# Prompt attention scores of dilated groups as two 64-row matmuls on queries read in place

## The chip, the cores and the metric

The kernel runs on one core of a Trainium2 chip. The metric is the device time of one execution in microseconds (us); for the kernel before it is the median of three runs.

## The reference

The program is one step of a small hybrid decoder with two layers, on a prompt of 1024 tokens and on 8 samples of 8 tokens. The first layer has three groups of dilated sliding-window attention (window and dilation 128 and 1, 512 and 4, 2048 and 16; 8 heads of 64 each), joined by their softmax denominators, beside a state-space layer; the second has sliding-window attention with sinks. Normalisations and a feed-forward block stand around both. What the change touches is the prompt's attention of the first layer:

```
def dilated_prompt(q, k, v, dilation, n_steps):
    # (1, T, H, 64) -> dilation sequences of T / dilation tokens
    o, m, l = banded_attn(split(q), split(k), split(v), n_steps)

def banded_attn(q, k, v, n_steps):      # blocks of 128 queries, own and previous key block
    s = einsum('nbqgrd,nbkgd->nbgrqk', qb, kb) * (hd ** -0.5)
    s = where(valid, s, NEG_INF); m = s.max(-1); pexp = exp(s - m); l = pexp.sum(-1)
    o = einsum('nbgrqk,nbkgd->nbqgrd', pexp, vb)
```

## The kernel before

Activations lie with features on the 128 partitions and tokens along the free dimension. Each of the five engines has one program of its own, and semaphores order them. Weights come through one buffer in 111 slots: a DMA on the SP queue, a split into a high and a low half on POOL, three matmuls for each product on PE.

For each of the three groups g0, g1, g2, PE computes values, queries and keys; ACT evicts queries and keys to `XA` (tiles 0 to 3 queries, 4 to 7 keys, two heads of 64 rows in each tile). Then `attend` runs on PE (L816 to L896), ACT (L1261 to L1326) and DVE (L1714 to L1786). It has eight tiles of 128 queries, and in each tile four steps of two heads. A tile has one or two key blocks of 128: in g0 all tiles but the first have two, in g1 they alternate (one, two), in g2 all have one. `prompt_cols` and `key_cols` pick the columns: contiguous in g0, with stride 4 in g1, with stride 8 in g2.

A step k goes through the engines as follows.

- ACT `stage` (from L1266, the copy at L1272): for each of the two heads it copies its 64 rows of the queries, times 1/8, into its own 128-column block of `QST`. The other 64 rows of that block are zero: DVE clears `QST` once (L1957). The staging of the next tile's queries stands between the steps of the present one; the first tile's four steps are staged at once at the start.
- PE `scores` (L822 to L833): it waits for the staged queries and for the mask of step k-2, then runs two matmuls of the full 128 rows (L831), the staged block against a whole key tile, into the two halves of one PSUM bank (bank k % 2).
- DVE: mask added into `sm` (L1755), row maximum, negated (L1760). At a tile's first step it also copies the sums of the last tile into `o_st` (L1726 to L1728), after waiting for the DMA that took the output before; at the third step it scales the last tile's output into `o_st` (L1740), and SP sends that to DRAM.
- ACT `exps` (L1287): exp with the maximum as bias, one instruction and one reading of the sum for each head; then `turned_out` of step k-2 (L1295), which evicts the transposed probabilities.
- PE `turn` of step k-2 (L842): transposes of the probabilities into bank 2 + k % 2; `weigh` of step k-3 (L856): the product with the values, into bank 4.

PE's order in a step is scores(k), turn(k-2), weigh(k-3); ACT's is exps(k), turned_out(k-2), stage. `over_tiles` (L277 to L300) runs the tiles as a hardware loop with its first and last ones written out. The second layer's attention uses the same function with 16 heads and its own staged buffer `QCST`. `block_outputs` (L1028 to L1040), in the state-space layer, alternates full-depth matmuls (L1033) with matmuls on 64 rows in two halves of the array and two banks (L1038); it is not touched.

In g2, SP loads the first keys, mask and values for the samples' attention between the tiles' outputs, after tiles 0, 2 and 4 (L463 to L472); the samples' attention follows the three groups, and waits for their last output.

Of the kernel before, what the change touches and what calls it, by code (L numbers as in the profile page):

```python
# [102 lines left out]
def build(nc, a):  # L103
# [14 lines left out]
    with ExitStack() as ctx:  # L118
# [68 lines left out]
        psum = ctx.enter_context(nc.psum_tensor("psum", [P, 8, 512], F32))  # L187
# [38 lines left out]
        def tiles(t, n):  # L226

            return t[:, :].rearrange("p (n c) -> p n c", n=n)
# [21 lines left out]
        QST, QCST = tiles(q_st, 8), tiles(qc_st, 16)  # L250
# [23 lines left out]
        def value_tile(g, i):  # L274
            return 2 * i[0] + i[1] if g == 1 else i

# [378 lines left out]
        def _(pe):  # L655
# [160 lines left out]
            def attend(g, heads, keys, vals):  # L816

                steps, per_kv = heads // 2, 1 if heads == H_A else 4
                staged = QST if heads == H_A else QCST

                def tile(i, nk, before, after):
                    K = key_cols(g, i, nk)(keys)  # L822

                    def scores(k):
                        pe.wait_ge(q_ready, n_q.add())
                        m = n_mask.add()
                        late(s_masked, m - 2)
                        for hh in range(2):
                            h = 2 * k + hh
                            kt = h // 2 if per_kv == 1 else h // 8  # L830
                            mm = pe.matmul(psum[:, k % 2, hh * 256:hh * 256 + nk * P], staged[:, h, :], K[:, kt],  # L831
                                           start=True, stop=True)
                        mm.then_inc(s_mm, 1)  # L833
# [58 lines left out]
                per = {n_q: steps, n_mask: steps, n_exp: steps, n_ptt: steps, n_pv: steps, n_o: 1}  # L892
                if heads == H_C:
                    per[lo] = 1
                over_tiles(pe, g, per, tile)
# [8 lines left out]
            for g in range(3):  # L904
# [26 lines left out]
                if g:  # L931
                    pe.wait_ge(v_turned, (0, 32, 48)[g])
# [264 lines left out]
        def _(act):  # L1197
# [63 lines left out]
            def attend(g, heads):  # L1261
                steps = heads // 2

                staged = QST if heads == H_A else QCST

                def stage(i, k):  # L1266

                    late(s_mm, n_s.add() - steps)
                    for par in range(2):
                        rows = 64 * (par if heads == H_A else (k // 2) % 2)  # L1270
                        q = prompt_cols(g, i)(XA[:, k:k + 1, :])[64 * par:64 * par + 64]
                        mm = act.activation(staged[rows:rows + 64, 2 * k + par:2 * k + par + 1, :], q, ACT.Copy,  # L1272
                                            scale=HEAD_DIM ** -0.5)
                    mm.then_inc(q_ready, 1)
# [79 lines left out]
            for g in range(3):  # L1354
# [15 lines left out]
                if g == 0:  # L1370
                    act.wait_ge(zeroed, 1)
# [34 lines left out]
            act.wait_ge(zeroed, 2)  # L1406
# [30 lines left out]
            act.wait_ge(zeroed, 3)  # L1437
# [20 lines left out]
            for layer in range(2):  # L1458
                if layer == 1:
# [12 lines left out]
                    act.wait_ge(zeroed, 4)  # L1472
# [143 lines left out]
        def _(dve):  # L1616
# [97 lines left out]
            def attend(g, heads):  # L1714
# [33 lines left out]
                def tile(i, nk, before, after):  # L1748
                    for k in range(steps):
# [5 lines left out]
                        dve.tensor_tensor(out, psum[:, k % 2, :].rearrange("p (h c) -> p h c", h=2)[:, :, 0:nk * P],  # L1755
                                          m.unsqueeze(1).broadcast_to([P, 2, nk * P]), ALU.add).then_inc(s_masked, 1)
# [200 lines left out]
            dve.memset(QST, 0.0).then_inc(zeroed, 1)  # L1957
# [457 lines left out]
```

## Time and profile before

| | us |
|---|---|
| median of three runs | 3750.82 |
| least and greatest | 3748.04, 3753.10 |
| profiled execution, own time | 3750.7 |
| profiled execution, span of its instructions | 3748.9 |
| PE busy | 3316.5 (88%) |
| PE weight loads busy | 3172.7 (85%) |
| DVE, ACT, POOL busy | 1485.0, 906.7, 989.7 |
| DMA | 323.01 MB, 24.8% of 16 engines |

PE is TensorE's matmul row and PEld its weight loads, which overlap; DVE is VectorE, ACT ScalarE, POOL GpSimd, SP the engine that issues the DMAs. The granted clock of TensorE is given as a share of 2.4 GHz; it has two levels, 1.0 and 0.5. A float32 matmul has two records of a load and a matmul each. Ends of matmuls are modelled, so the distance from one start to the next tells more than a record's length.

### The profile page before, as it was taken

The page shows a single profiled execution, that of the slowest core. Times are in us where ns is not written, and L with a number is a line of the kernel's source. Part 1 is how long each engine was busy: PE and PEld are TensorE (multiplying, and loading weights), DVE is VectorE, ACT ScalarE, POOL GpSimd, SP SyncE. Part 2 cuts the span into 40 slices and gives each one's busy share as a digit, 9 for nine tenths or more (in the row PEclk, how much of TensorE's full clock was granted, in tenths as well). Part 3 has the DMA queues.
Part 4 walks back from the last instruction along what each step waited for, and adds up shares of the span by engine and source line. Part 5 has one row for each costly group of instructions (what it writes and reads, how often), then busy time and mean ns, then how long its engine had stood idle before and what let it go on. Part 6 is the DMA issues. An engine that isn't in the chain of part 4 may idle for free.

```text
span 3748.9 us, 50836 instructions
## 1 busy us (share of the span) xinstructions
PE 3316.5 (88%) x21025; PEld 3172.7 (85%) x21025; DVE 1485.0 (40%) x1852; ACT 906.7 (24%) x1876; POOL 989.7 (26%) x226
## 2 busy tenths in 40 slices
PE   4978999984478899999999799887889999999978
PEld 4977987983357799999999698876879999999968
DVE  7714013033452533333334762265154333333474
ACT  3106125061031410000001531275141000000151
POOL 3321230310002233333333333200123333333321
PEclk8989999987688999999999899999799999999989
DMA  2221210348921112222225121100111222222411
GB/s 97 103 72 49 90 66 21 118 151 257 279 70 72 48 72 92 92 92 92 92 92 182 39 78 42 53 1 31 60 66 54 78 78 78 78 78 78 156 36 60
DMA packets 84128, 323.01 MB, mean 86 GB/s; under 512 B 19033, under 2 KB 32153, under 8 KB 66073
## 3 DMA queue, kind: packets, MB, share of 16 engines
q1 hardware_dynamic: 84000, 321.18, 24.8%
q8 instruction: 96, 1.57, 0.2%
q14 instruction: 32, 0.25, 0.0%
HBM read 271.98 MB, written 105.23 MB: 101 GB/s over the span
## 4 chain that ended last, share of the span: by engine, by line
issue 36%; POOL 21%; PE 20%; DMA 15%; DVE 3%; ACT 3%; SPq 2%; POOLq 0%; ACTq 0%; DVEq 0%
DMA w_raw<-in_wall 12%; POOL w_lo L643 12%; PE psum L759 11%; POOL w_hi L641 9%; PE psum L784 3%; PE psum L831 2%; PE psum L856 1%; ACT pr L1287 1%; PE psum L700 1%; DMA v_sb<-in_v 1%; SPq L542 1%; PE psum L1033 1%; PE psum L1038 1%; PE psum L958 1%; PE psum L734 0%
## 5 line engine op out<-in xcount | busy, mean ns | idle before, releaser
L641 POOL TENSOR_TENSOR w_hi<-w_raw,param 128x2184 fp32r<-128x2184 f32 x111 | 427.8, 3854 | 2703.9 <-PE psum L759 2132.0
L759 PE MATMUL psum<-h_hi,w_hi 128*128 128x364 f32 x2832 | 630.7, 331 | 42.1 <-ACT xa L1245 22.8
L759 PE MATMUL psum<-h_lo,w_hi 128*128 128x364 f32 x2544 | 567.1, 331 | 8.3 <-DVE h_hi L1678 8.3
L643 POOL TENSOR_TENSOR w_lo<-w_raw,w_hi 128x2184 fp32r<-128x2184 f32 x111 | 561.7, 5060 | 8.7
L759 PEld LDWEIGHTS psum<-h_hi,w_hi 128*128 128x128 f32 x2832 | 497.6, 190 | 43.8 <-ACT xa L1245 23.1
L759 PE MATMUL psum<-h_hi,w_lo 128*128 128x364 f32 x2304 | 512.4, 331 | 0.0
L2198 DVE TENSOR_TENSOR xa<-xa,psum 128x1092 f32<-128x1092 f32 x256 | 330.4, 1291 | 339.6 <-PE psum L759 339.4
L759 PEld LDWEIGHTS psum<-h_lo,w_hi 128*128 128x128 f32 x2544 | 445.0, 190 | 9.3 <-DVE h_hi L1678 9.0
L759 PEld LDWEIGHTS psum<-h_hi,w_lo 128*128 128x128 f32 x2304 | 403.3, 190 | 0.0
L1560 ACT ACTIVATE tmp<-tmp 128x1092 f32<-128x1092 f32 x64 | 71.5, 1118 | 1261.9 <-DVE tmp L2182 1261.9
L759 PE MATMUL psum<-hid_lo,w_hi 128*128 128x364 f32 x1536 | 339.4, 329 | 0.0
L759 PE MATMUL psum<-hid_hi,w_lo 128*128 128x364 f32 x1536 | 339.4, 329 | 0.0
L759 PE MATMUL psum<-hid_hi,w_hi 128*128 128x364 f32 x1536 | 337.6, 328 | 0.0
L2182 DVE SCALAR_TENSOR_TENSOR tmp<-psum,sq 128x1092 f32<-128x1092 f32 x64 | 82.7, 1295 | 544.0 <-PE psum L759 514.0
L1755 DVE TENSOR_TENSOR sm<-psum,mask 128x512 f32<-128x512 f32 (+1 forms) x160 | 94.4, 590 | 511.0 <-PE psum L831 506.9
L759 PEld LDWEIGHTS psum<-hid_hi,w_hi 128*128 128x128 f32 x1536 | 267.2, 188 | 0.0
L759 PEld LDWEIGHTS psum<-hid_lo,w_hi 128*128 128x128 f32 x1536 | 266.9, 188 | 0.0
L759 PEld LDWEIGHTS psum<-hid_hi,w_lo 128*128 128x128 f32 x1536 | 265.8, 188 | 0.0
L784 PE MATMUL psum<-w_hi,h_hi 128*128 128x256 f32 x648 | 185.1, 286 | 23.2 <-DVE h_lo L1638 21.5
L784 PE MATMUL psum<-w_hi,h_lo 128*128 128x256 f32 x648 | 184.1, 284 | 0.0
L1287 ACT ACTIVATE pr<-sm,stat 128x256 f32<-128x256 f32 (+1 forms) x320 | 147.1, 460 | 95.2 <-DVE stat L1760 49.1
L784 PE MATMUL psum<-w_lo,h_hi 128*128 128x256 f32 x576 | 164.1, 285 | 0.0
(313 smaller groups left out, 4467.5 us busy)
## 6 DMA issues: line engine op xcount, KB each, us to landing
w_raw<-in_wall SPq DMA_DIRECT2D x111, 1092.0 KB, 5.0
kt_sb<-in_kt SPq DMA_DIRECT2D x16, 1024.0 KB, 10.9
out_ovs<-in_v SPq DMA_DIRECT2D x8, 2032.0 KB, 15.6
x_keep<-xa SPq DMA_DIRECT2D x2, 4368.0 KB, 11.8
xd_late<-x_keep SPq DMA_DIRECT2D x2, 4368.0 KB, 14.0
out_oks<-in_kt SPq DMA_DIRECT2D x8, 1008.0 KB, 8.2
out_ovs<-in_v SPq DMA_DIRECT2D x8, 1008.0 KB, 8.8
og<-o_st SPq DMA_DIRECT2D x24, 264.0 KB, 2.0
```

The lines of the kernel that those rows point to most:

```text
L542: sp.dma_start(DM[16 * k:16 * k + 16, :, :], s5_k[:, :, 16 * k:16 * k + P]).then_inc(d_in, 16)
L641: pool.tensor_tensor(w_hi[b][:, :], w_raw[:, :], param[:, C_ONE:C_ONE + 1].broadcast_to([P, SLOT]), ALU.mult).then_inc(hi_made, 1)
L643: pool.tensor_tensor(w_lo[b][:, :], w_raw[:, :], w_hi[b][:, :].bitcast(F32), ALU.subtract).then_inc(split, 1)
L700: mm = pe.matmul(UNIT[m][:, c, :], w[:, kc, m * P:m * P + P], x[:, kc, c * CH:(c + 1) * CH], start=kc == 0 and w is WH and x is XH, stop=k ...
L759: mm = pe.matmul(UNIT[s][:, c, :], w[:, kc, cols], x[:, kc, c * CH:(c + 1) * CH], start=first, stop=last)
L784: mm = pe.matmul(psum[:, 3 * s + c, 0:256], x[:, kc], w[:, kc, :], start=kc == 0 and x is XH and w is WH, stop=kc == KC - 1 and x is XL)
L831: mm = pe.matmul(psum[:, k % 2, hh * 256:hh * 256 + nk * P], staged[:, h, :], K[:, kt], start=True, stop=True)
L1287: mm = act.activation(pr[:, o:o + nk * P], sm[:, o:o + nk * P], ACT.Exp, bias=stat[:, h:h + 1], accum_out=stat[:, 16 + h:17 + h])
L1560: act.activation(TMP[:, m, :], TMP[:, m, :], ACT.Square).then_inc(act_own, 1)
L1755: dve.tensor_tensor(out, psum[:, k % 2, :].rearrange("p (h c) -> p h c", h=2)[:, :, 0:nk * P], m.unsqueeze(1).broadcast_to([P, 2, nk * P]) ...
L2182: dve.scalar_tensor_tensor(chunked(TMP[:, m, :]), UNIT[m], 0.0, chunked(rs2), ALU.max, ALU.mult).then_inc(free[m], 1)
L2198: dve.tensor_tensor(chunked(XA[:, m, :]), chunked(XA[:, m, :]), UNIT[m % 2], ALU.add).then_inc(free[m % 2], 1)
```

## The change

The prompt attention of the three dilated groups no longer stages its queries. The two matmuls of a step take 64 rows each, one the upper and one the lower half of the array, with the queries read from `XA` in place as the stationary operand, strided in g1 and g2. They write two PSUM banks, 0 and 1 in even steps and 5 and 6 in odd ones. The factor 1/8 moves into the mask, which becomes a scalar_tensor_tensor. PE waits no more for staged queries in these groups, DVE no longer clears `QST`, and the counts of the semaphore `zeroed` go down by one. PE's program for these groups is written out over the eight tiles instead of looping; ACT, DVE and SP keep their loops. In g0 PE waits for `k_evict`, since bank 6 is now used. The second layer's attention stays as it is.

```
+        def over_tiles_written_out(g, tile):
+            order = [divmod(t, 2) for t in range(8)] if g == 1 else range(8)
+            nk = [1 + t % 2 if g == 1 else min(t + 1, 2 - g // 2) for t in range(8)]
+            steps = list(zip(order, nk))
+            for t, (i, n) in enumerate(steps):
+                tile(i, n, steps[t - 1] if t else None, steps[t + 1] if t < 7 else None)
...
                     def scores(k):
-                        pe.wait_ge(q_ready, n_q.add())
+                        if heads == H_C:
+                            pe.wait_ge(q_ready, n_q.add())
                         m = n_mask.add()
                         late(s_masked, m - 2)
                         for hh in range(2):
                             h = 2 * k + hh
-                            kt = h // 2 if per_kv == 1 else h // 8
-                            mm = pe.matmul(psum[:, k % 2, hh * 256:hh * 256 + nk * P], staged[:, h, :], K[:, kt],
-                                           start=True, stop=True)
+                            if heads == H_A:
+                                rows = slice(64 * hh, 64 * hh + 64)
+                                mm = pe.matmul(psum[:, 5 * (k % 2) + hh, 0:nk * P],
+                                               prompt_cols(g, i)(XA[:, k:k + 1, :])[rows, 0], K[rows, k],
+                                               start=True, stop=True)
...
-                over_tiles(pe, g, per, tile)
+                if heads == H_A:
+                    over_tiles_written_out(g, tile)
...
-                if g:
+                if g == 0:
+                    pe.wait_ge(k_evict, 8)
+                else:
                     pe.wait_ge(v_turned, (0, 32, 48)[g])
                 attend(g, H_A, XA[:, 4:8, :], V)
...
                 def stage(i, k):
+                    if heads == H_A:
+                        n_s.add()
+                        return
...
-                if g == 0:
-                    act.wait_ge(zeroed, 1)
                 attend(g, H_A)
...
-                        dve.tensor_tensor(out, psum[:, k % 2, :].rearrange("p (h c) -> p h c", h=2)[:, :, 0:nk * P],
-                                          m.unsqueeze(1).broadcast_to([P, 2, nk * P]), ALU.add).then_inc(s_masked, 1)
+                        m = m.unsqueeze(1).broadcast_to([P, 2, nk * P])
+                        if heads == H_A:
+                            dve.scalar_tensor_tensor(out, psum[:, 5 * (k % 2):5 * (k % 2) + 2, 0:nk * P],
+                                                     HEAD_DIM ** -0.5, m, ALU.mult, ALU.add).then_inc(s_masked, 1)
...
             dve.wait_ge(t_parked, 16)
-            dve.memset(QST, 0.0).then_inc(zeroed, 1)
```

## Rows read from the trace of the kernel before

**Rows 1.** Windows of the three stages: length, PE PEld DVE ACT POOL busy, clock, DMA

```profile
300.60:388.70 88.10, 73.02 (x488) 63.96 (x488) 48.83 (x96) 66.15 (x224) 7.48 (x2) 0.98 0.12 42
537.20:627.70 90.50, 82.02 (x416) 60.11 (x416) 42.82 (x96) 68.66 (x224) 7.52 (x2) 0.94 0.14 50
776.20:855.40 79.20, 66.14 (x320) 58.57 (x320) 34.49 (x96) 61.91 (x224) 7.50 (x2) 0.74 0.52 168
```

**Rows 2.** Chain of waits inside g0: start us, length us, what ended last

```profile
356.47 0.93 PE psum L831 x4
357.43 0.70 DVE sm L1755
358.15 0.70 DVE stat L1760
359.97 0.49 ACT pt L1295
360.69 1.10 PE psum L856 x8
```

**Rows 3.** Timeline of the same turn in g0: start, length, engine, instructions

```profile
357.23 0.60 PE L842 MATMUL psum<-ident,pr 128*128 128x128 f32 x4
358.51 1.08 PE L831 MATMUL psum<-xa,q_st 128*128 x4
358.88 0.51 ACT L1287 ACTIVATE pr<-sm,stat 128x256 f32<-128x256 f32 x1 [1.27 <-DVE stat L1760]
```

**Rows 4.** Timeline of ACT at the start of g1

```profile
537.26 3.56 ACT L1272 ACTIVATE q_st<-xa 64x128 f32<-64x128 f32 x8
```

**Rows 5.** Timeline of g1: first scores of three tiles, staging, maximum, exponential

```profile
557.55 1.12 PE L831 MATMUL psum<-xa,q_st 128*128 x4
567.24 2.01 PE L831 MATMUL psum<-xa,q_st 128*128 x4
579.18 1.15 PE L831 MATMUL psum<-xa,q_st 128*128 x4
580.63 1.75 ACT L1272 ACTIVATE q_st<-xa 64x128 f32 x4
581.17 0.42 DVE L1760 TENSOR_REDUCE stat<-sm 128x2 f32<-128x256 f32 x1
582.40 0.40 ACT L1287 ACTIVATE pr<-sm,stat 128x128 f32<-128x128 f32 x1
```

**Rows 6.** Timeline of PE in g2 at the low clock: scores, then transposes

```profile
804.88 1.23 PE L831 MATMUL psum<-xa,q_st 128*128 x4
805.93 0.61 PE L842 MATMUL psum<-ident,pr 128*128 128x128 f32 x2
```

**Rows 7.** Timeline of PE in the block outputs of the state-space layer

```profile
1073.10 0.71 PE L1038 MATMUL psum<-ca,hv 64*128 64x128 f32 x8
1073.75 0.71 PE L1033 MATMUL psum<-d_mat,ut 128*128 128x128 f32 x4
1074.39 0.71 PE L1038 MATMUL psum<-ca,hv 64*128 64x128 f32 x8
```

**Rows 8.** Two groups of the page: line, operation, count, busy us, mean ns

```profile
L2198 DVE TENSOR_TENSOR xa<-xa,psum 128x1092 f32<-128x1092 f32 x256 | 330.4, 1291 | 339.6 <-PE psum L759 339.4
L2182 DVE SCALAR_TENSOR_TENSOR tmp<-psum,sq 128x1092 f32<-128x1092 f32 x64 | 82.7, 1295 | 544.0 <-PE psum L759 514.0
```

**Rows 9.** Weight loads by tile: with stride 32, contiguous; ns least, median, greatest

```profile
L1007 PEld LDWEIGHTS psum<-ident,ub x32: 186/196/231, 1015.9 to 1020.7; 128*128 128x128 f32 x32
L831 PEld LDWEIGHTS psum<-xa,q_st x384: 186/192/338, 301.4 to 849.8; 128*128 128x128 f32 x192
```

**Rows 10.** Timeline of SP and DVE in g2

```profile
828.40 0.43 SPq L400 DMA_DIRECT2D sm_sb<-in_smask  x1
844.07 0.17 DVE L1726 COPY o_st<-stat 128x8 f32<-128x8 f32 x1 [4.32 <-DMA og<-o_st]
```

**Rows 11.** Window at the end of g2, columns as in rows 1

```profile
842.00:857.00 15.00, 7.69 (x40) 7.11 (x40) 4.94 (x15) 5.13 (x22) 0.00 (x0) 0.70 0.12 45
```

More of the change, by code:

```diff
@@ L249, in build @@
         G = param[:, 0:80].rearrange("p (l k c) -> p l k c", l=2, k=5)
-        QST, QCST = tiles(q_st, 8), tiles(qc_st, 16)
+        QCST = tiles(qc_st, 16)
         UNIT = [psum[:, 3 * s:3 * s + 3, 0:CH] for s in range(2)]
@@ L829, in scores @@
                             h = 2 * k + hh
-                            kt = h // 2 if per_kv == 1 else h // 8
-                            mm = pe.matmul(psum[:, k % 2, hh * 256:hh * 256 + nk * P], staged[:, h, :], K[:, kt],
-                                           start=True, stop=True)
+                            if heads == H_A:
[4 more added lines that the diff above has]
+                            else:
+                                mm = pe.matmul(psum[:, k % 2, hh * 256:hh * 256 + nk * P], QCST[:, h, :], K[:, h // 8],
+                                               start=True, stop=True)
                         mm.then_inc(s_mm, 1)
@@ L890, in tile @@
                             outputs_turned()
-                per = {n_q: steps, n_mask: steps, n_exp: steps, n_ptt: steps, n_pv: steps, n_o: 1}
-                if heads == H_C:
-                    per[lo] = 1
-                over_tiles(pe, g, per, tile)
+                if heads == H_A:
+                    over_tiles_written_out(g, tile)
+                else:
+                    over_tiles(pe, g, {n_q: steps, n_mask: steps, n_exp: steps, n_ptt: steps, n_pv: steps, n_o: 1, lo: 1},
+                               tile)
                 pe.wait_ge(o_made, n_o.at)
@@ L1262, in attend @@
                 steps = heads // 2
-                staged = QST if heads == H_A else QCST
                 def stage(i, k):
+                    if heads == H_A:
+                        n_s.add()
+                        return
                     late(s_mm, n_s.add() - steps)
                     for par in range(2):
-                        rows = 64 * (par if heads == H_A else (k // 2) % 2)
+                        rows = 64 * ((k // 2) % 2)
                         q = prompt_cols(g, i)(XA[:, k:k + 1, :])[64 * par:64 * par + 64]
-                        mm = act.activation(staged[rows:rows + 64, 2 * k + par:2 * k + par + 1, :], q, ACT.Copy,
+                        mm = act.activation(QCST[rows:rows + 64, 2 * k + par:2 * k + par + 1, :], q, ACT.Copy,
                                             scale=HEAD_DIM ** -0.5)
@@ L1754, in tile @@
                         m = mask[:, 2 * P:3 * P] if g == 2 else mask[:, 2 * P - nk * P:2 * P]
-                        dve.tensor_tensor(out, psum[:, k % 2, :].rearrange("p (h c) -> p h c", h=2)[:, :, 0:nk * P],
-                                          m.unsqueeze(1).broadcast_to([P, 2, nk * P]), ALU.add).then_inc(s_masked, 1)
+                        m = m.unsqueeze(1).broadcast_to([P, 2, nk * P])
+                        if heads == H_A:
+                            dve.scalar_tensor_tensor(out, psum[:, 5 * (k % 2):5 * (k % 2) + 2, 0:nk * P],
+                                                     HEAD_DIM ** -0.5, m, ALU.mult, ALU.add).then_inc(s_masked, 1)
+                        else:
+                            dve.tensor_tensor(out, psum[:, k % 2, :].rearrange("p (h c) -> p h c", h=2)[:, :, 0:nk * P],
+                                              m, ALU.add).then_inc(s_masked, 1)
                         if k == 0 and before:
```

8 lines of the change are left out of this document (4 added, 4 removed).

## The prediction

> **What bounds the kernel now.** The whole kernel is held by TensorE, but the change lives in three short stages, the prompt attention of the three dilated groups (g0, g1, g2), so only these are read. The first view is the table of windows [rows 1]: the stages last 88.1, 90.5 and 79.2 us, 257.8 us together, and no engine is busy all through. PE comes nearest with 73.02, 82.02 and 66.14 us, but that busy time contains the modelled ends of matmuls. The granted clock is 0.98 and 0.94 in g0 and g1: all but some 3.5 and 11 us at the 2.4 GHz level. In g2 it is 0.74: half of the stage at 1.2 GHz.
>
> The second view is the chain of waits inside g0 [rows 2]. It runs in a circle: scores of a step (L831, 0.93 us), mask (L1755, 0.70), row maximum (L1760, 0.70), two exponentials with their sums on ACT (from 358.87 to 359.97, 1.1), the eviction of an older transposed block (L1295, 0.49, and 0.23 to PE), its product with the values (L856, 1.10), and then the next scores, at 361.79. PE's program puts the product of step k-3 ahead of the scores of step k+1, and ACT's program puts the exponentials of step k-1 ahead of the eviction of step k-3. So one turn of the circle is two steps: 361.79 - 356.47 = 5.32 us. A group has 32 steps, 16 turns; 88.1 / 16 = 5.5 us is the mean turn with its fill and ends. The engines alone would be faster: from the start of a step's transposes over its product to the next scores PE takes 358.51 - 357.23 = 1.28 us [rows 3], with the scores 2.21 a step, 4.42 a turn. Each turn holds the scores once, not twice.
>
> **g0, scores.** The change makes the two matmuls of a step 64 rows deep, in two halves of the array and two PSUM banks. The trace of before has that shape elsewhere: in the block outputs, lines L1033 and L1038 alternate [rows 7]. Two full-depth matmuls (four records) take 1074.39 - 1073.75 = 0.64 us; four matmuls of 64 rows (eight records) take 1073.75 - 1073.10 = 0.65 us, with the same 128 columns. So two halves run in the time of one, and a pair costs half of what it did. Scores fall from 0.93 to 0.46 us. 15 of the 16 turns of g0 have this size (the first tile has one key block): 15 x 0.46 = 7.0 us. The turn stays the limit: about 5.1 us, against 3.5 for PE, 2 x 2 x 0.72 plus 0.5 = 3.4 for DVE, and 3.0 for ACT.
>
> The same rows show a change between 128 and 64 rows every 0.65 us without a gap. The Trainium skill, TensorEngine Tiling (Array Packing), Key Properties, says that changing the tiling mode drains TensorE; by these rows the drain costs nothing that can be seen, and the sum goes by the rows. The case in which it costs is a rival below.
>
> **Staging.** It drops 192 ACT instructions. In g0 they cost nothing but at the start: behind them ACT still waits 1.27 us for DVE [rows 3]. In g1 the queries are read with a stride and a pair costs 0.86 us; two pairs fall together at a tile's start, run from 580.63 to 582.38, and the exponential begins at 582.40 although its maximum was there at 581.17 + 0.42 = 581.59 [rows 5]: 0.8 us late, which I take as 0.75 in each of the four tiles with one key block. In g2 the same block stands before each tile; between 0 (as in g0) and 0.75 I take 0.15 a tile, since there the maximum comes later against the block than in g1. At each group's start eight stagings precede the first exponential: in g1 3.56 us from 537.26 [rows 4]. Without them scores (0.5), mask and maximum (0.45 each) and their hand-overs put it 1.7 us after 537.26, so 1.85 us are gained; the same in g2, and 1.05 in g0, whose stagings are shorter. The memset of the cleared buffer stands ahead of the stage in DVE's program, which then waits for the first scores: 0.
>
> **g1, scores.** Keys are read with a stride there. A step's four records span 2.01 us with 256 columns and 1.12 to 1.15 with 128 [rows 5]; less the 0.15 by which the 1.08 of [rows 3] exceeds the chain's 0.93 [rows 2], scores cost 1.86 and 0.97. A tile with two key blocks takes 579.18 - 567.24 = 11.94 us, one with a single block 567.24 - 557.55 = 9.69 [rows 5]. In the first PE is itself nearly the limit. Halved, its scores are 0.93; the circle then holds, with 0.93 + 0.72 + 0.72 + 1.1, 0.6 for the eviction and 0.9 for a product of one or two key blocks, 5.0 us a turn against 5.97 now: 1.9 us a tile, 7.6 for four. In the second each of two turns loses 0.48, and 0.75 of staging goes: 1.7 a tile, 6.9 for four. Together 14.5 us at the high clock, and 1.85 at the start.
>
> **g2.** A turn loses half of 805.93 - 804.88 = 1.05 us at the low level [rows 6], of 0.97 at the high one: 0.5, so 1.0 a tile, with 0.15 of staging 1.15, 9.2 for eight tiles, and 1.8 at the start. A DMA gives part back: after tile 4 the SP queue issues the sample's mask and values, from 828.40 on, tile 5's output goes behind them, and DVE stands still for it until 844.07 [rows 10]. These 15.6 us stay whatever the engines do, so what is saved on the 1.6 tiles between, about 1.8 us, only makes the wait longer. Downstream nothing swallows the rest: DMA share is 0.12 in the 15 us at the end of g2 [rows 11], and the DMA-heavy sample stage behind it starts when g2's last output lands.
>
> **The clock.** Shorter scores leave PE less to do per us. g2, with the smallest matmuls, is already at the low level for half of its time, g0 and g1 hardly ever [rows 1]. I take g0 as unchanged. In g1 I take a third at the low level: a step with transposes and products of two key blocks is then PE's own, 0.53 + 2.56 = 3.1 us (double of the 1.28 of [rows 3]) against 2.0, 4 us a tile, and 0.7 us for a tile of the other kind; a third of 4 x 4.7 is 6.3. In g2 I take all of it at the low level, 0.5 us a tile more than the mix of today: 2.4 in the parts not held by the DMA.
>
> **Edits with one answer.** The mask becomes a scalar_tensor_tensor with the scale in it: the page has both forms at 1092 columns, 1295 against 1291 ns [rows 8], so 0; bounds 0 and, if 0.1 us in each of 48 turns, 5 us. The stationary operand is read with stride 4 or 8: loads with stride 32 took 196 ns in the median, the contiguous ones of the staged queries 192 [rows 9]: 0. PE's program is written out: the block outputs of [rows 7] are written out too and run without a gap, so fetching costs nothing, and the turns of the loop may be gained, at most the 0.23 us ahead of a product [rows 2] once a tile: 0 to -5, taken as 0. k_evict counts copies that DVE makes before it comes to the stage: 0. Behind PE's dropped wait for staged queries stood the transposes and products of older steps; they now wait for the mask alone.
>
> **Sum.** g0 -7.0 - 1.05 = -8.0; g1 -14.5 + 6.3 - 1.85 = -10.0; g2 -9.2 + 1.8 + 2.4 - 1.8 = -6.8. Together -24.8 us, set against the profiled execution's 3750.7 us (span 3748.9 and 1.8 around it, next to the median 3750.82): 3726 us. With no clock lost, and 2 us of loop turns, it is -35.5: 3715; with half of g1 low, 0.05 us for each switch and each mask: 3738.
>
> **Rivals.**
> - The clock falls in g0 too, and in all of g1: slower. For it: g2, the lightest stage, keeps falling [rows 1]. Against it: g0's transposes and products stay twice as large as g2's. At the low level PE is the limit in g0: 0.93 + 2.56 = 3.49 us a step against 2.55 in my forecast and 2.75 now; 32 x 0.74 - 1.05 = +22.6 us against now. g1 low throughout is 12 against 9.7 us in one kind of tile and 9.6 against 11.9 in the other, so only its start's -1.85 is left; g2 -6.8. Sum +14: 3765. It decides when 26 of g0's 32 steps run low (24.8 / 0.94), with g1 as forecast; 16 to 24 of them give 3741 to 3749.
> - The halves don't overlap where keys are strided. The operands of [rows 7] are contiguous; if the strided read is limited for the array as a whole, scores keep their 0.97 and 1.86 us. Then g0 -8.0, g1 -4 x 0.75 - 1.85 = -4.9, g2 -1.2 - 1.8 = -3: 3735. If no pair overlaps at all, g0 keeps only its start: 3742.
> - Each switch of depth waits for the array to empty. The tail of the last record is 0.07 us in [rows 7] (0.71 less 0.64) and 0.15 in the scores (1.08 less 0.93, [rows 2, 3]); at 0.11, one or two in each of 48 turns are 5 to 10 us: 3731 to 3736. The page's rule on draining (the Trainium skill, TensorEngine Tiling (Array Packing), Key Properties) says this; the seamless cadence of [rows 7] speaks against it.
> - The change doesn't do what it says to the circle: a link that I can't see (the mask on two banks, say) grows by what the scores lose, and only starts are left: 3746.
>
> **How the numbers follow.** About 0.2% (7.5 us) is what a measurement of this kernel can tell from no change: below 3743.3 is faster, above 3758.3 slower. Forecast 0.62; no overlap 0.12 (strided 0.08, none 0.04); draining 0.07: these are faster, 0.81. The clock low in part of g0 0.08 and the unseen link 0.04 are within 0.2%: 0.12. The clock low in all of g0 and g1, 0.07, is slower. The range takes in the forecast's own 3715 to 3738, draining and both kinds of no overlap, and half of the partly low clock: 3713 to 3747.
>
> **What would show it.** In the changed profile the four records of a step's scores should span about 0.5 us in g0 and g2 and 0.95 in g1's larger tiles; a turn in g0 should be near 5.1 us; ACT should have no L1272 in these stages; the stages should last about 80, 80 and 72 us with granted clocks near 1.0, 0.8 and 0.55; DVE's wait for the output's DMA in g2 should grow from 4.3 to about 6 us. The forecast is wrong if records of the two halves follow one another, if g0's granted clock is under 0.9, or if a turn in g0 stays above 5.4 us at the high clock.

## The result, and the profile after

The change makes the kernel slower. The median is 3787.32 us (12 executions, 3756.15 to 3793.90) against 3750.57 us for the kernel before beside it (12, 3747.16 to 3756.52); the ratio is 1.0072, 95% interval 1.0044 to 1.0099. The forecast was 3726 us, in 3713 to 3747. The ratios here are of means. The changed kernel's executions come at two times some 30 us apart, five of these 12 at 3756 to 3763 us and seven at 3785 to 3794, and what divides them is part of the explanation.

The profiled execution took 3793.68 us (span 3791.9). The windows of its three stages, with the columns of [rows 1], from the end of ACT's last eviction to the end of DVE's last output:

```profile
299.32:416.02 116.70, 114.62 (x488) 91.08 (x488) 49.49 (x96) 48.76 (x161) 7.51 (x2) 0.51 0.09 32
566.21:665.94 99.73, 96.86 (x416) 77.27 (x416) 43.20 (x96) 43.62 (x160) 7.53 (x2) 0.52 0.13 45
815.82:893.16 77.34, 70.59 (x320) 57.06 (x320) 34.58 (x96) 36.36 (x160) 7.53 (x2) 0.52 0.51 172
```

The last column but two is what to see: the granted clock is 0.51 and 0.52 in all three stages, 1.2 GHz almost throughout, where it was 0.98, 0.94 and 0.74. g0 grew by 28.6 us and g1 by 9.2; g2 lost 1.9. ACT is busy for 17 to 26 us less a stage, as the staging went, and the stages don't show it. The chain of waits in g0 (start, length, what ended last) answers [rows 2]:

```profile
355.40 1.16 PE psum L840 x4
356.56 1.04 PE psum L855 x4
357.61 1.60 PE psum L869 x8
359.20 1.16 PE psum L840 x4
```

DVE and ACT have left the chain. Scores (L840), transposes (L855) and product (L869) of PE follow one another, and a step takes 359.20 - 355.40 = 3.80 us, where it was 2.75. The timeline of PE and its weight loads (PEld) at the same place answers [rows 3]:

```profile
356.49 1.11 PE L855 MATMUL psum<-ident,pr 128*128 128x128 f32 x4
356.49 0.71 PEld L855 LDWEIGHTS psum<-ident,pr 128*128 128x128 f32 x4 [0.65 <-issue]
357.40 1.81 PE L869 MATMUL psum<-v_sb,pt 128*128 128x64 f32 x8
357.19 1.83 PEld L869 LDWEIGHTS psum<-v_sb,pt 128*128 128x128 f32 x8
```

The product's first load starts 0.21 us ahead of its matmul, beside the transposes. The transposes' first load starts with its own matmul: behind the 64-row scores nothing is loaded ahead. In ACT's timeline the first exponential stands at

```profile
298.24 1.08 ACT L1261 ACTIVATE xa<-psum 128x1092 f32 x1 [10.90 <-PE psum L767]
301.02 0.40 ACT L1304 ACTIVATE pr<-sm,stat 128x128 f32<-128x128 f32 x1 [1.69 <-DVE stat L1780]
...
565.13 1.08 ACT L1261 ACTIVATE xa<-psum 128x1092 f32 x1 [10.90 <-PE psum L767]
568.24 0.40 ACT L1304 ACTIVATE pr<-sm,stat 128x128 f32<-128x128 f32 x1 [2.02 <-DVE stat L1780]
```

so it begins 1.70 us after the eviction in g0 and 2.03 in g1. Eight stagings stood there before, 3.56 us of them in g1 [rows 4].

| part of 3793.68 - 3750.7 = 43.0 us | us |
|---|---|
| g0, g1, g2 | +28.6, +9.2, -1.9 |
| ahead of g0 | -1.2 |
| between g0 and g1, and g1 and g2 (the first values still run at 1.2 GHz: clock 0.50 from 416 to 420, 1.00 before) | +1.7, +1.4 |
| behind g2 | +5.2 |

The last line can't be put down to the change: from g2's end to the end of the span it is 2887.9 us (the changed kernel again, below) to 2905.8 us in the 17 traces of this study, 2893.5 before. So a single profile is compared here by its stages, and whole times by their intervals.

### The profile page after: what moved, and what is told of

It is laid out like the page before. It is cut to its first block, busy times and chain, and to the rows that moved or that the text cites. A ratio compares the mean times of both kernels' runs of the same rounds, so it can differ in the third digit from the quotient of the medians.

```text
span 3791.9 us, 50096 instructions
## 1 busy us (share of the span) xinstructions
PE 3382.3 (89%) x21025; PEld 3218.9 (85%) x21025; DVE 1484.6 (39%) x1851; ACT 838.7 (22%) x1684; POOL 993.5 (26%) x226
## 4 chain that ended last, share of the span: by engine, by line
issue 35%; PE 23%; POOL 21%; DMA 15%; SPq 3%; DVE 3%; ACT 1%; POOLq 0%; ACTq 0%; DVEq 0%
DMA w_raw<-in_wall 12%; POOL w_lo L651 12%; PE psum L767 11%; POOL w_hi L649 9%; PE psum L869 3%; PE psum L792 3%; PE psum L840 2%; PE psum L855 2%; DMA v_sb<-in_v 1%; PE psum L708 1%; SPq L404 1%; SPq L550 1%; PE psum L1049 1%; PE psum L1054 1%; PE psum L742 0%
## 5 line engine op out<-in xcount | busy, mean ns | idle before, releaser
L1772 DVE SCALAR_TENSOR_TENSOR sm<-psum,mask 128x256 f32<-128x256 f32 (+1 forms) x96 | 52.4, 546 | 522.8 <-PE psum L840 520.8
```

The lines of the kernel that those rows point to most:

```text
L1772: dve.scalar_tensor_tensor(out, psum[:, 5 * (k % 2):5 * (k % 2) + 2, 0:nk * P], HEAD_DIM ** -0.5, m, ALU.mult, ALU.add).then_inc(s_masked, 1)
```

## The experiments

Theory A is the first rival of the prediction: the clock falls and PE becomes the limit. Against it stand B, that the written-out program of PE costs the time, and C, that matmuls of 64 rows cost more than they save whatever the clock is. A came to be split as the runs went on (A1, A2, D1, D2). `...` marks what is left out of an edit. All measured times:

| kernel | median us (least to greatest, executions) | ratio to before, 95% interval |
|---|---|---|
| half_cols | 3745.28 (3737.47 to 3756.01, 10) | 0.9981 (0.9969 to 0.9993) |
| before_written_out | 3753.80 (3742.32 to 3758.94, 10) | 0.9997 (0.9985 to 1.0009) |
| fill_all | 3738.14 (3731.37 to 3773.34, 5) | 0.9955 (0.9938 to 0.9971) |
| fill_first | 3748.96 (3743.42 to 3754.39, 10) | 0.9988 (0.9978 to 0.9997) |
| fill_mid | 3761.08 (3752.67 to 3767.16, 8) | 1.0022 (1.0012 to 1.0032) |
| full_depth, full_depth_again | 3730.50 (2), 3741.85 (3736.66 to 3746.35, 5) | 0.9940 (0.9920 to 0.9960), 0.9959 (0.9945 to 0.9973) |
| switch_only | 3823.89 (3821.07 to 3837.29, 4) | 1.0203 (1.0182 to 1.0224) |
| tiny_full | 3795.11 (3741.50 to 3798.32, 10) | 1.0066 (1.0027 to 1.0105) |
| after_again | 3788.58 (3749.09 to 3792.38, 5) | 1.0094 (1.0079 to 1.0110) |
| start_only | 3792.43 (3754.94 to 3798.89, 9) | 1.0095 (1.0070 to 1.0119) |
| mixed | 3748.54 (3745.18 to 3753.41, 10) | 0.9984 (0.9975 to 0.9994) |
| kick | 3738.04 (3729.82 to 3760.60, 10) | 0.9967 (0.9949 to 0.9985) |
| best | 3743.34 (3732.29 to 3744.23, 11) | 0.9974 (0.9965 to 0.9983) |
| best_128 | 3742.63 (3737.76 to 3750.39, 8) | 0.9970 (0.9959 to 0.9980) |

### The program alone: before_written_out

```diff
...
-                over_tiles(pe, g, per, tile)
+                if heads == H_A:
+                    over_tiles_written_out(g, tile)
+                else:
+                    over_tiles(pe, g, per, tile)
```

> The kernel before with one part of the change alone: PE's program of the dilated groups is written out over the eight tiles. Theory B (the longer program costs time, in fetching its instructions): the stages grow, by up to the 28 and 9 us by which g0 and g1 grew, and the whole is 3765 to 3790 us. Theory A (the clock): the scores are as long as before, so the stages and clocks are those of before and the whole is 3745 to 3753 us; the loop's turns are worth 0 to 5 us.

The ratio is 0.9997, stages 86.3, 89.9 and 76.3 us at clocks of 0.98, 0.94 and 0.76. B is out.

### Shorter scores without row groups: half_cols

```diff
-                            mm = pe.matmul(psum[:, k % 2, hh * 256:hh * 256 + nk * P], staged[:, h, :], K[:, kt],
+                            w = P if heads == H_A else nk * P
+                            mm = pe.matmul(psum[:, k % 2, hh * 256:hh * 256 + w], staged[:, h, :], K[:, kt, 0:w],
...
```

> The kernel before with one edit: in the dilated groups the scores of a tile with two key blocks are computed for the first block alone, and the mask reads these 128 columns twice (so the second block's scores are left out, and the result means nothing). Depth of the matmuls, staged queries, banks and the looping program stay. So the scores of g0 and of half of g1 cost half, as after the change, without its row groups. Theory A (shorter scores leave TensorE too little to do, its clock falls to 1.2 GHz and PE becomes the limit): the granted clock of g0 falls from 0.98 to under 0.8, g0 lasts 100 to 115 us instead of 88.1, the whole 3760 to 3785 us. Theory C (the 64-row matmuls and the change of depth cost the time by themselves): the clock stays above 0.9, g0 lasts about 81 us, the whole 3735 to 3743 us.

```profile
298.98:385.48 86.50, 70.15 (x488) 63.76 (x488) 48.77 (x96) 66.01 (x224) 7.51 (x2) 0.88 0.12 43
535.55:622.77 87.22, 76.89 (x416) 68.99 (x416) 43.03 (x96) 68.84 (x224) 7.54 (x2) 0.80 0.15 52
```

Neither forecast came. The clock falls, to 0.88 and 0.80, so shorter scores do cost clock; but in this trace it comes back, no execution is above 3756.01 us, and the kernel is a little faster. Shorter scores alone don't explain 0.51.

### More work for PE: fill_all, fill_first, fill_mid

In fill_all, `COND` is `True`; in fill_first it is `value_tile(g, i) < 2`, in fill_mid `g == 0 and value_tile(g, i) in (4, 5)`.

```diff
                             turn(steps - 2 + k, before[1])
+                        if heads == H_A and COND:
+                            pe.matmul(psum[:, 7, 0:256], ident[:, :], mask[:, 0:256], start=True, stop=True)
                         if k >= 3:
```

> The changed kernel with one full-depth matmul of 256 columns more in every step of the dilated groups, from constants into PSUM bank 7, which nothing reads; it stands between the transposes and the product, where PE waits for ACT. It takes 0.46 us at the high level of the clock (half of the 0.93 of the old scores), about what the scores lost. Theory A: the clock comes back to 0.95 or more in g0 and 0.85 or more in g1, g0 lasts 79 to 84 us, g1 80 to 88, g2 70 to 79, the whole 3725 to 3742 us, faster than both kernels although TensorE does more. Theories B and C (program, switch of depth, strided operand): the added work can only cost; 32 steps of 0.46 to 0.93 us in each group, the whole 3790 to 3850 us.

> As the kernel with one more 256-column matmul in each step, but only in the first two of the eight tiles of each group. Theory A in its plain form (each step for itself does too little): the clock is high in the first quarter of g0 and falls behind it, g0 lasts 100 to 110 us, the whole 3770 to 3785 us. Theory A with a level that holds itself (at the high level the steps are short enough to keep it, at the low level they are not): once the stage begins high it stays so, g0 lasts 79 to 86 us, the whole 3730 to 3750 us. Theories B and C: slower than the changed kernel by 8 steps of 0.5 to 0.9 us in each group, 3790 to 3810 us.

Windows of the stages, fill_all first, then g0 of fill_first and four stretches of its g1:

```profile
299.13:381.50 82.37, 79.02 (x552) 61.44 (x552) 49.83 (x96) 48.73 (x161) 7.51 (x2) 1.00 0.13 46
530.02:624.89 94.87, 91.52 (x480) 70.10 (x480) 43.30 (x96) 43.58 (x161) 7.53 (x2) 0.84 0.13 48
773.41:869.53 96.12, 95.14 (x384) 77.46 (x384) 34.68 (x96) 36.90 (x161) 7.51 (x2) 0.52 0.43 139
```

```profile
300.77:382.40 81.63, 70.18 (x504) 53.22 (x504) 49.83 (x96) 48.71 (x161) 7.52 (x2) 1.00 0.13 46
...
531.00:555.00 24.00, 24.00 (x136) 17.27 (x137) 12.73 (x30) 13.08 (x51) 7.40 (x2) 1.00 0.35 119
555.00:561.00 6.00, 5.18 (x27) 3.19 (x28) 4.33 (x10) 3.21 (x14) 0.00 (x0) 1.00 0.12 46
561.00:567.00 6.00, 6.00 (x27) 4.49 (x28) 3.39 (x6) 2.93 (x10) 0.00 (x0) 0.55 0.11 45
567.00:624.00 57.00, 56.53 (x247) 46.60 (x246) 22.45 (x53) 24.52 (x87) 0.00 (x0) 0.50 0.05 20
```

Adding work makes the kernel faster: A, against B and C. In g0 work in two tiles is enough: the clock is 1.00 to the stage's end, six tiles after the last added matmul. So in g0 the level holds itself. In g1 it doesn't: the level is lost soon after the added work stops, and then stays lost. The profiled execution of fill_all (3773.34 us; the ratio leaves it out) shows the other side: in g2 PE is busy for 95.14 of 96.12 us, the clock stays at 0.52, and g1 (94.87 us) and g2 miss what was expected of them. The clock of that whole execution is 0.933, of the other four 0.942 to 0.947, so this kernel too has a longer time in some executions.

> The changed kernel with the 256-column matmul more only in the steps of tiles 4 and 5 of g0; g1 and g2 are as changed. It tells whether the level of the clock holds itself. Theory A with a level that holds itself: g0 begins at 1.2 GHz as in the changed kernel (four tiles at 14 to 15 us each), comes to 2.4 GHz in tile 4 or 5, and stays there in tiles 6 and 7 without any added work; g0 lasts 95 to 103 us, tiles 6 and 7 about 10 us each. Theory A in its plain form (each step for itself does too little): the clock falls again in tiles 6 and 7, g0 lasts 107 to 115 us. If the level can't be left once it is low: g0 lasts 119 to 125 us.

This run's profile didn't tell what it was made for. In its profiled execution (3752.67 us) g0 came back to 1.00 at 314, in the second tile, before the tiles with added work; g0 took 83.0 us, g1 98.9 at 0.51, g2 77.2. That is the changed kernel's shorter time, and the next run has the same without any addition. But none of the eight executions is near 3790 us (3767.16 at most), where the changed kernel has 11 of 17: by these odds the added work keeps g0 from staying low to its end. When the other seven came back isn't shown.

### The changed kernel once more: after_again

> The changed kernel as it is, for a trace of its other execution time and its spread beside the others of this call. Theory A with a level that holds itself: its executions fall into two times some 30 us apart, near 3758 and 3790 us; in the shorter one g0 comes back to 2.4 GHz after its first tiles and lasts 81 to 86 us, while g1 (97 to 101) and g2 (76 to 79) are as slow as in the longer one.

The windows of g0's beginning and rest: the long execution (3793.68 us) of the first profile, and the short one (3749.09 us) of this run.

```profile
304.70:313.50 8.80, 8.78 (x35) 5.99 (x34) 4.39 (x9) 3.68 (x16) 2.21 (x1) 0.50 0.34 127
313.50:416.00 102.50, 101.72 (x433) 82.38 (x432) 41.80 (x79) 41.90 (x132) 0.00 (x0) 0.50 0.05 19
```

```profile
304.30:313.00 8.70, 8.68 (x35) 5.96 (x34) 4.39 (x9) 3.58 (x16) 2.17 (x1) 0.50 0.38 130
313.00:381.00 68.00, 59.69 (x433) 45.67 (x432) 40.84 (x78) 41.86 (x132) 0.00 (x0) 0.99 0.07 29
```

For some 8.7 us the two do the same at 1.2 GHz. Then one comes back and the other doesn't: 82.9 us for g0 against 116.7. The difference, 33.8 us, is about the distance between the two times. g1 (100.2 us at 0.51) and g2 (78.6 at 0.53) are low in both. With the 12 executions above, 6 of 17 come back, 11 don't; their clocks over the whole execution part in the same way, 0.922 to 0.925 in the six and 0.909 to 0.913 in the eleven.

### What keeps the level low: full_depth, switch_only, tiny_full

full_depth is the changed kernel with full-depth matmuls of half the columns: the scores stream as long as in the changed kernel, from the same operands into the same banks, without a change between 64 and 128 rows. The mask is a plain addition here, over the same columns twice.

```diff
-                                rows = slice(64 * hh, 64 * hh + 64)
-                                mm = pe.matmul(psum[:, 5 * (k % 2) + hh, 0:nk * P],
-                                               prompt_cols(g, i)(XA[:, k:k + 1, :])[rows, 0], K[rows, k],
+                                w = nk * P // 2
+                                mm = pe.matmul(psum[:, 5 * (k % 2) + hh, 0:w],
+                                               prompt_cols(g, i)(XA[:, k:k + 1, :])[:, 0], K[:, k, 0:w],
...
```

> The changed kernel with full-depth matmuls of half the columns in the dilated groups in place of the two 64-row ones: both heads' rows together against half of the key columns, and the mask reads these columns twice, without the scale (so the scores mean nothing). The time in which the scores stream is the same as in the changed kernel, queries are read in place, nothing is staged, and no change between 64 and 128 rows is left. Theory A1 (the shorter scores alone keep the clock low): the clock of g0 is about 0.5 and g0 lasts 105 to 115 us. Theory A2 (it takes the change of depth as well, whose exposed weight loads stretch the step at the low level to 3.80 us where 3.49 was worked out): the clock dips at the start and comes back, as in the kernel with staged queries and half the columns; g0 lasts 77 to 90 us at a clock above 0.85.

```profile
299.00:379.74 80.74, 65.50 (x488) 60.25 (x488) 48.50 (x96) 48.47 (x161) 7.51 (x2) 0.92 0.13 46
528.20:611.56 83.36, 76.74 (x416) 72.29 (x416) 43.04 (x96) 43.56 (x160) 7.54 (x2) 0.77 0.15 54
760.09:837.56 77.47, 71.59 (x320) 67.09 (x320) 34.71 (x96) 36.66 (x160) 7.53 (x2) 0.51 0.51 172
```

This is near the forecast's stage table (80, 80, 72 us at 1.0, 0.8, 0.55) but for g2, and the two executions, 3728.71 and 3732.29 us, are near its 3726. That it met the whole so closely is in part luck. In full_depth_again the stages are the same (80.8, 83.6, 78.0 us), but its five executions take 3736.66 to 3746.35, two of them above what was expected. Of the 17.6 us between the two profiled executions 15.8 stand behind g2. What the forecast described is shorter scores without the change of depth. To see that the change of depth is the difference, switch_only puts it back with next to no work, behind each step's scores; tiny_full is its control, with the same matmul at full depth (`ident[:, :]` and `mask[:, 0:8]`).

```diff
                         mm.then_inc(s_mm, 1)
+                        if heads == H_A:
+                            pe.matmul(psum[:, 7, 0:8], ident[0:64, :], mask[0:64, 0:8], start=True, stop=True)
```

> The kernel with full-depth scores of half the columns (queries in place, two banks) with one matmul of 64 rows and 8 columns more behind each step's scores, into bank 7, which nothing reads: a change of depth and back in every step, with next to no streaming. It tells whether the change of depth alone makes the difference between that kernel (3730 us, g0 80.7, g1 83.4 us, clock 0.92 and 0.77) and the changed one. Theory A2 (the change of depth exposes weight loads, the step at 1.2 GHz grows from 3.4 to about 3.8 us, and so the low level lasts): the distance from scores to transposes at the low level grows from 0.96 to 1.15 us or more, g1 lasts 92 to 102 us at a clock near 0.5, g0 is high in some executions and low throughout in others, the whole 3750 to 3795 us. Theory A3 (not the change, but the half-filled array itself counts as less work for the clock): g0 and g1 stay within 3 us of 80.7 and 83.4, the whole 3731 to 3738 us.

> The control for the kernel with one change of depth more: the same added matmul of 8 columns behind each step's scores, but of the full 128 rows, so that no change of depth is left, only the added matmul and its weight load, about 0.45 us at the low level (two records of a load at 0.22 to 0.23). Theory D1 (what counts is how long a step takes at the low level for the columns that it streams: 3.4 us comes back to 2.4 GHz, 3.8 us in some executions, 4.13 us in none): the step is about 3.8 us, and this kernel behaves as the changed one does, g1 at 0.5 for nearly all of its 95 to 101 us, g0 low throughout in some executions, the whole 3750 to 3795 us. Theory D2 (it takes the change of depth, loads in plain sequence don't do it): the clock comes back in g0 and g1 as without the added matmul, the whole 3731 to 3742 us.

> The kernel with full-depth scores of half the columns again, for more executions of it: with two of them known, that it always comes back from the low level isn't settled. Theory A2 and D1: all of its executions within 3724 to 3742 us. If its two executions were lucky: some near 3760 to 3775 us, with g0 low throughout.

One step of g0's second tile at 1.2 GHz in PE's timeline, from scores to scores, its product still with one key block: full_depth, the changed kernel, switch_only (L848 is the added matmul). In the first two `...` stands for the transposes and the product.

```profile
310.06 1.17 PE L840 MATMUL psum<-xa 128*128 128x128 f32 x4
...
312.62 1.17 PE L840 MATMUL psum<-xa 128*128 128x128 f32 x4
```

```profile
310.59 1.23 PE L840 MATMUL psum<-xa 64*128 64x256 f32 x4
...
313.54 1.23 PE L840 MATMUL psum<-xa 64*128 64x256 f32 x4
```

```profile
308.87 1.17 PE L840 MATMUL psum<-xa 128*128 128x128 f32 x4
309.96 0.59 PE L848 MATMUL psum<-mask,ident 64*128 64x8 f32 x2
310.49 1.11 PE L857 MATMUL psum<-ident,pr 128*128 128x128 f32 x4
311.40 0.95 PE L871 MATMUL psum<-v_sb,pt 128*128 128x64 f32 x4
312.14 1.17 PE L840 MATMUL psum<-xa 128*128 128x128 f32 x4
```

| the same step at 1.2 GHz | us | g0 came back (by the executions' times and clocks) |
|---|---|---|
| half_cols, 310.40 to 312.96 | 2.56 | 10 of 10 |
| full_depth | 2.56 | 7 of 7 |
| tiny_full, 311.04 to 313.92 | 2.88 | 4 of 10 |
| the changed kernel | 2.95 | 6 of 17 |
| switch_only | 3.27 | 0 of 4 |

The change of depth costs 2.95 - 2.56 = 0.39 us a step at the low level, and 3.27 - 2.88 = 0.39 as well where switch_only is set beside tiny_full. switch_only came out slower than both of its forecasts: g0 125.6 us at 0.51, g1 124.5 at 0.56, the whole 3821 us or more. It is D1 that stands, not D2: tiny_full has no change of depth, only a matmul and its loads that make the step 0.32 us longer, and falls into two times as the changed kernel does (though in its profiled execution g1 is at 0.66, not 0.5). So a longer step is enough to make the low level last, without a change of depth; the change of depth is how this kernel came by it. Only the profiled executions show g0's level directly. The others are told by their time and their clock over the whole execution: in tiny_full 0.924 to 0.930 in four, of which one took 3770.24 us, and 0.909 to 0.912 in the six near 3795. That the odds follow the step's length rests on these five lengths.

### Versions with added work: start_only, mixed, kick, best, best_128

In kick, best, best_128 and start_only, `fill(512)` (two matmuls of 256 columns) stands twice ahead of the stage and once in each of the first two steps, in kick in all three groups, in the others in g0 and g1. `REST` is 0 in start_only; in best it is 256 in g0's first two tiles and all of g1; best_128 has 128 for g1's tiles with two key blocks; kick adds 256 in all of g2. The wait `u.all_free` moves behind the first addition.

```diff
-                u.all_free(pe)
...
+                for _ in range((2, 2, 0)[g]):
+                    fill(512)
+                u.all_free(pe)
...
+                        if heads == H_A:
+                            fill(512 if g < 2 and not before and k < 2 else REST)
```

> The same with the added matmuls only ahead of g0 and g1 and in their first two steps, none later. Theory A, where the start decides and the level holds itself: g0 at the high level from its first step, 79 to 82 us in every execution; g1, whose strided steps fell back when the added work ended after two tiles, falls within its first two tiles and lasts 93 to 99 us; g2 76 to 78; the whole 3745 to 3757 us without executions near 3790. If the start doesn't decide: g0 falls to the low level in some of them, and these take 3780 us or more.

> Row groups and queries read in place in g0 alone, with one 256-column matmul more a step in its first two tiles; g1 and g2 keep the staged queries and full-depth matmuls of the kernel before (TensorE's program is written out in all three). Theory A: g0 lasts 81 to 83 us at a clock of 0.98 or more, as in the kernel with the added work in the first two tiles; g1 89 to 91 and g2 75 to 80 us as before, so 5 to 8 us less than the kernel before, 3743 to 3749 us. Theory C (64-row matmuls cost more than they give, even at the high level): no gain over the kernel before, 3750 us or more.

> The changed kernel with more work put where TensorE idles at the start of each dilated group: four matmuls of 256 columns ahead of the stage, where it waits for ACT's last eviction, two in each of the first two steps, then one a step (in g0 in the first two tiles only, in g1 and g2 in all). Theory A: all three groups begin at 2.4 GHz; g0 lasts 79 to 82 us, g1 80 to 90, g2 70 to 78, the clock is above 0.95, 0.8 and 0.8, the whole 3722 to 3738 us. If a start at the high level isn't enough for the strided groups: g1 90 to 95 and g2 77 to 96 us at a clock of 0.5 to 0.65, the whole 3745 to 3775 us.

> The changed kernel with added 256-column matmuls where they held the clock, and none in g2: four ahead of g0 and g1 and two in each of their first two steps; one a step in g0's first two tiles and in all of g1. Theory A: g0 81 to 83 us and g1 84 to 86 us, both at a clock of 0.98 or more; g2, without the added work that took 86 us at the low level, 76 to 78 us; the whole 3727 to 3735 us, faster than the kernel before by 0.5 to 0.7%.

> The version with added matmuls in g0 and g1, with 128 columns in place of 256 where a tile of g1 has two key blocks: there TensorE is nearly the limit, at 10.7 us a tile. If the high level stands this: four tiles shorter by 0.5 to 0.9 us each, g1 81 to 83 us at a clock of 0.98 or more, 2 to 4 us less than with 256 columns. If not: g1 falls to the low level and lasts 90 us or more, the whole 3745 us or more.

Windows of two stretches of start_only's g0, then the stages of best:

```profile
305.00:311.00 6.00, 3.81 (x26) 2.72 (x28) 3.26 (x8) 3.95 (x17) 2.32 (x1) 1.00 0.42 143
311.00:317.00 6.00, 6.00 (x28) 4.78 (x28) 3.44 (x5) 2.99 (x12) 0.00 (x0) 0.52 0.23 91
```

```profile
300.75:382.92 82.17, 71.49 (x511) 54.08 (x509) 49.26 (x96) 48.76 (x161) 7.51 (x2) 1.00 0.13 46
531.43:616.31 84.88, 83.26 (x487) 62.57 (x485) 43.17 (x96) 43.64 (x161) 7.53 (x2) 1.00 0.15 53
764.84:842.51 77.67, 70.85 (x320) 57.20 (x320) 34.58 (x96) 36.36 (x161) 7.52 (x2) 0.51 0.50 171
```

start_only refutes the guess that the start decides. g0 begins at 2.4 GHz and falls at 311, after steps in which PE was busy 3.81 of 6.00 us; eight of nine executions are the long ones. best differs from it in g0 only by 256 columns in each later step of the first two tiles, and stays at 1.00 there. So what must be carried over is the light beginning, the first tile with its single key block and the second; the runs don't part these two.

mixed gains what g0 alone can give: 81.6 us there at 1.00, 89.4 and 77.4 in g1 and g2. kick, best and best_128 hold g0 and g1 (84.9, 84.9, 86.2 us) and beat the kernel before by 0.26 to 0.33%, and so the changed one. fill_all beats it by 0.45% without its execution at 3773.34 us, by 0.25% with it. Their intervals overlap, so which is best stays open. best's stages came as expected, but not its whole (3743.34 us, where 3727 to 3735 were expected). best_128 didn't give its 2 to 4 us: its clock in g1 is 0.96, with a fall on the way. Work of this size didn't hold g2: in kick the clock falls 29 us in, and g2 lasts 85.9 us, 8 us more than without. best leaves that work out, and its total doesn't show those 8 us: 0.9974 against 0.9967. In its profiled execution they are there, but g0 begins 2.2 us later than in kick's and 4.8 us more stand behind g2, both within the spread of the 17 traces. Whether more than that spread is behind it stays open.

## Why the prediction was wrong

**The step that failed** is "I take g0 as unchanged" in the part on the clock, and behind it "a third" for g1. The cases were set out, and the right one was given 0.07: clock low in all of g0 and g1, 3765 us. The row to be read differently is the clock of g0 [rows 1]. 0.98 meant that the kernel before lost the level for some 3.5 us at g0's start and won it back, as two windows of its trace show:

```profile
300.60:305.30 4.70, 3.76 (x18) 3.43 (x18) 2.53 (x6) 4.49 (x18) 4.62 (x2) 0.65 0.53 139
305.30:309.00 3.70, 2.78 (x19) 2.26 (x18) 1.47 (x4) 3.60 (x16) 2.86 (x1) 0.99 0.00 0
```

I counted these 3.5 us as small and didn't ask what wins the level back, and whether the shorter step still would. In the changed kernel it didn't in 11 of 17 executions: g0 stood at 0.51 for its 116.7 us in the profiled one, under the 0.9 that was set as a sign of being wrong. g1 was low not for a third but nearly throughout, at 0.52 and 0.51 in both traces. Without the change of depth g0 came back in 7 of 7 (full_depth).

**Mis-sized in that rival.** A low step of g0 came out at 3.80 us, not 3.49; g0 +28.6 us, not +22.6; g1 +9.2, not -1.9 (its tiles with two key blocks and one at 13.67 and 10.61 us from output to output, not 12 and 9.6); g2 -1.9, not -6.8. Together that is 36 us from the stages instead of 14. The 0.39 us a step of the next point are 12.5 us over the 32 steps of a stage, by estimate, and cover the 6.0 and 11.1 us by which g0 and g1 are off; what is off in g2 is told below.

**The change of depth isn't free.** I took it as free by the seamless cadence of [rows 7]. The price was inside that cadence: at 2.4 GHz, with full-depth neighbours, four such records of 128 columns take 0.50 us in full_depth, where [rows 7] show 0.64. PE's timelines of fill_first and full_depth in g0, scores to scores without a wait:

```profile
340.91 1.10 PE L869 MATMUL psum<-v_sb,pt 128*128 128x64 f32 x8 [0.90 <-ACT pt L1314]
341.94 0.70 PE L840 MATMUL psum<-xa 64*128 64x256 f32 x4
342.57 0.42 PEld L855 LDWEIGHTS psum<-ident,pr 128*128 128x128 f32 x4 [0.33 <-issue]
344.00 0.70 PE L840 MATMUL psum<-xa 64*128 64x256 f32 x4
...
345.86 1.07 PE L869 MATMUL psum<-v_sb,pt 128*128 128x64 f32 x8 [0.57 <-ACT pt L1314]
```

```profile
340.34 0.66 PE L840 MATMUL psum<-xa 128*128 128x128 f32 x4
340.84 0.60 PE L855 MATMUL psum<-ident,pr 128*128 128x128 f32 x4
342.11 0.66 PE L840 MATMUL psum<-xa 128*128 128x128 f32 x4
```

2.06 us of PE a step against 1.77, and 2.20 before. Of the 0.46 us that the scores were to save PE, 0.29 are taken back. I put them down to the two changes of depth in a step; at this level no run parts these from other costs of the 64-row pair, as switch_only does at 1.2 GHz. The rule of the Trainium skill, TensorEngine Tiling (Array Packing), Key Properties, that a change of tiling mode drains TensorE, agrees with these rows; the rival that followed it was right in kind, and too small (0.11 us for one or two changes in each of 48 turns).

**Right.** At the high level the forecast of g0 nearly holds: 81.6 us against 80.1 (fill_first, with work added in two tiles), with a turn of 345.86 - 340.91 = 4.95 us from product to product against 5.1. Some of that is luck: g0 of before_written_out is at 86.3 us already, so by one trace each 1.8 of the 6.5 us came with the written-out program, which the sum took as 0. The two halves overlap, on strided keys too, though not to a half: in g1 scores to transposes with two key blocks take 1.21 us, where they took 1.83 before (567.24 [rows 5] to 569.07) and 0.93 was forecast. kick at a clock of 1.00, and the changed kernel at 0.50:

```profile
577.59 1.28 PE L845 MATMUL psum<-xa 64*128 64x256 f32 x4
578.80 0.44 PE L860 MATMUL psum<-ident,pr 128*128 128x128 f32 x2
...
596.72 1.28 PE L840 MATMUL psum<-xa 64*128 64x256 f32 x4
597.92 0.69 PE L855 MATMUL psum<-ident,pr 128*128 128x128 f32 x2
```

The starts gained 1.0 us in g0, 1.6 in g1 and 1.7 in g2, against 1.05 and 1.85. The mask with its scale takes 0.69 us as the plain addition did, and the written-out program costs nothing (ratio 0.9997).

**g2** stayed at 76 to 79 us in all kernels without added work in it. The forecast halved a circle of waits; at 1.2 GHz PE is the limit here too, a tile takes 8.77 us in the changed kernel where nothing else is waited for, and DVE waits for an output's DMA four times for 1.2 to 1.6 us, not once for 6.

## What to carry to other kernels

Before making matmuls cheaper in a loop that waits on other engines, read the granted clock of that stretch, work out the step at both levels, and ask whether the step at the low level is still one that comes back; a stage at 0.98 that dips at its start says that the level is lost and won there. Where the level is lost, a few full-depth matmuls into a bank that nobody reads can cost less than the level: with them the whole kernel here is 0.26 to 0.33% faster than before, without them 0.7% slower. Row groups next to full-depth matmuls paid for each change of depth here, about 0.15 us at 2.4 GHz and 0.2 at 1.2 (halves of 0.29 and 0.39); a cadence that alternates the two already holds that price.

## What the runs showed of the hardware

- One kernel on one core has two times 30 us apart, because TensorE's level, once low, can last for a whole stage of over 100 us, and in two executions alike for 8.7 us it came back in one and not in the other.
- PE busy through the stage by the profile's count doesn't bring the level back: 114.62 of 116.70 us in g0 of the changed kernel, 95.14 of 96.12 in g2 of fill_all, at 0.51 and 0.52. The Trainium skill, TensorE: Matmul & The Clock Gate, What's actually happening, has the clock set by how busy TensorE has been; by these rows the profile's busy time can't be taken for that.
- Scores on keys read with a stride take the same at both levels: in g1 1.21 us for two key blocks at 1.00 (kick) and 1.20 at 0.50 (the changed kernel), so there a higher clock gains nothing on them.
